# Eighteen more activation tiles of a two-block layer turned by the DMA crossbar

## The chip, the core and the metric

The kernel runs on one core of one Trainium2 chip. The metric is the device time of one execution in microseconds (us), the median of several. Each engine (PE = TensorE, ACT = ScalarE, DVE = VectorE, POOL = GpSimd, SP = SyncE, whose queue issues the DMAs) takes its instructions strictly in order and waits for the others by semaphores.

## The reference, cut to what matters

Two transformer-like blocks on 256 tokens of width 2048, all in float32.

```python
# first block: convolution + neighbourhood attention, then an MLP
proj = rms_norm(x, pre_mix_g) @ w_in                      # a, gate, q, k, v
mix  = concat([conv_group(a, gate), attention(q, k, v, rpb)]) @ w_out
x    = x + rms_norm(mix, post_mix_g)
f    = square(relu(rms_norm(x, pre_mlp_g) @ w_up)) @ w_down
x    = x + rms_norm(f, post_mlp_g)
# second block: mLSTM beside latent attention
proj = rms_norm_2(x, norm_g) @ w_in_2    # q_a,k_a,v_a,o_a,i_a,f_a,z_a,c_q,c_kv,k_r,z_b,g_a,g_b
qk_a = silu(causal_depthwise_conv(concat([q_a, k_a]), conv_w))      # 4 taps along tokens
h_a  = rms_norm_2(mlstm_chunkwise(q_a, k_a, v_a, i_a, f_a), mlstm_norm_g)
y_a  = (sigmoid(o_a) * h_a * silu(z_a)) @ w_a
q_b  = rope(rms_norm_2(rms_norm_2(c_q, q_lat_g) @ w_uq))
k_b, v_b = from(rms_norm_2(c_kv, kv_lat_g) @ w_ukv, k_r)
y_b  = (causal_attention(q_b, k_b, v_b) * silu(z_b)) @ w_b
y    = sigmoid(g_a) * y_a + sigmoid(g_b) * y_b
out  = x + y @ w_out_2
```

## The kernel before, in words

**Products.** Every large product has the activations (256 tokens, as two tiles of 128) stationary and streams weights. For float32 accuracy each operand is split in a high and a low part, and three products are added: `hi*whi`, `hi*wlo`, `lo*whi` (L594 to L596). The weights come in 732 units of 512 KB. A unit is loaded by SP into one of 4 buffers `raw` (L2215), ScalarE makes `whi` (L907), VectorE makes `wlo = raw - whi` (L1457), both in rings of 5, and TensorE multiplies the unit with 12 matmuls of 128x512 (two 128-row chunks, two token tiles, three products). A stripe is 512 output columns: 8 units where the sum runs over 2048 rows, 4 where over 1024.

**Order.** There is no scheduler at run time. Time is laid out in slots, two to a unit; `E("name")` is the slot in which stripe "name" has been summed. Each engine's program is made of generators ("sides"), one per kind of work; a side yields the slot at which its next piece stands, and the engine's program is the merge by slot. The splits of unit v stand at the slot in which unit v-5 has been multiplied (`slots_and_splits`, L507), since only then a place in the ring is free. So on VectorE and ScalarE an instruction that waits holds all splits behind it, and SP holds all loads behind a waiting transfer (a load of unit u+4 waits for the splits of unit u).

**Turning.** A stripe's result has tokens on the partitions, but the next product needs the features there. The tile is turned in 128x128 blocks. Most are turned on TensorE: `turn` (L569) makes four transposes (L573) into one PSUM bank, ScalarE reads the bank for the high part, VectorE for the low part. Only the 16 tiles of the MLP (`up`) are turned by the DMA crossbar, which takes 2-byte words: VectorE cuts the tile in its two 16-bit halves (L1720, two int16 copies), SP issues four DMA_TRANSPOSE (L2251), VectorE joins the halves (L1726, two int16 copies).

**The places concerned.** `qk2` are four stripes of 8 units, q_a and k_a of the mLSTM. Each is scaled by ScalarE (L883), turned, copied by ScalarE into `PRE` (L1160), convolved on VectorE (L1811 two and L1814 six instructions a pair of heads), passed through tanh (L1164) and combined (L1819). Beside it `row_side` works on the mLSTM's gates (VectorE L1840 to L1850, ScalarE L1183 to L1185). `ml` is the gated mLSTM result (4 tiles), `lat` the two latents, `ao` the attention's output (4 tiles), `yt` the sum of both branches (4 tiles, stripes `yb10` to `yb13` of 4 units each, the last product before `out0` to `out3`): VectorE adds the gated product (L2092, L2096), and makes the low part (L2102) from the turned tile.

Of the kernel before, what the change touches and what calls it, by code (L numbers as in the profile page):

```python
# [16 lines left out]
P = 128  # L17
# [170 lines left out]
def two_blocks(nc, d, out):  # L188
    with ExitStack() as ctx:
# [112 lines left out]
        PRE = [ar(12320 + 518 * i, 518).rearrange("p (k n) -> p k n", k=2) for i in range(2)]  # L302
        ROWS = [AR[0:8, 9260 + 256 * i:9516 + 256 * i] for i in range(9)]
# [12 lines left out]
        SG.append(ar(15360, 1024).rearrange("p (t n) -> p t n", t=2))  # L316
        at_p = [ar(16384 + 384 * i, 384) for i in range(3)]
# [39 lines left out]
        def sems(*names):  # L357
# [8 lines left out]
        ao_t, sm_t, row_t, row_n, ml_s, ml_o, ml_t = sems(  # L366
            "ao_t", "sm_t", "row_t", "row_n", "ml_s", "ml_o", "ml_t")
# [36 lines left out]
        yt_t = Later(x_t, 32)  # L404
# [120 lines left out]

        def na_parts():
# [13 lines left out]
        use += [(E(f"qk2{k // 2}") + 2 + 4 * (k % 2), "qk2", k) for k in range(8)]  # L540
        use += [(E(("cq", "ckv")[k // 2]) + 1 + k % 2, "lat", k) for k in range(4)]
        use += [(E(f"uqr{k // 2}") + 12 + 2 * (k % 2), "qr", k) for k in range(4)]
# [3 lines left out]
        use += [(AO0[k // 2] + 2 * (k % 2), "ao", k) for k in range(8)]  # L546
        TBK = {(name, k): 2 + i % 2 for i, (_, name, k) in enumerate(sorted(use))}
# [11 lines left out]
        def pe(e):  # L559
# [132 lines left out]
            def qk2_side():  # L692
                for n in range(4):
                    for pair in range(2):
                        yield E(f"qk2{n}") + 2 + 4 * pair
                        b = bank(TBK["qk2", 2 * n + pair], (qk2_p, 2 * n + pair + 1))
                        q.wait_ge(qk2_e, n + 1)
                        turn(b, SG[(0, 2, 3, 0)[n]], pair).then_inc(qk2_t.sem, 1)

# [24 lines left out]
            def ml_side():  # L724
                for n in range(4):
# [3 lines left out]
                    parts += [(ML0[2 * n + 1] + 8 + 2 * pair, "t", pair) for pair in range(2)]  # L729
                    for slot, part, h in sorted(parts):  # L730
# [8 lines left out]
                        elif part == "o":  # L739
# [8 lines left out]
                        else:  # L748
                            b = bank(h, (ml_h, 2 * n + h + 1), (ml_l, 2 * n + h + 1))
                            q.wait_ge(ml_x, 2 * n + 2)  # L750
                            turn(b, SG[n % 2], h).then_inc(ml_t, 1)

            def lat_side():
                for w, name in enumerate(("cq", "ckv")):
                    for pair in range(2):
                        yield E(name) + 1 + pair
                        b = bank(TBK["lat", 2 * w + pair], (lat_h, 2 * w + pair + 1), (lat_l, 2 * w + pair + 1))
                        q.wait_ge(lat_e, w + 1)
                        turn(b, SG[w], pair).then_inc(lat_t.sem, 1)
# [32 lines left out]
            def at_side():  # L792
                for slot, part, i in at_parts():
# [14 lines left out]
                    elif part == "t":  # L808
                        b = bank(1, (at_c, i + 1))
# [4 lines left out]
                    else:  # L814
                        b = bank(1, (at_x, i + 1))
# [7 lines left out]
            def ao_side():  # L823
                for n in range(4):
                    for pair in range(2):
                        yield AO0[n] + 2 * pair
                        b = bank(TBK["ao", 2 * n + pair], (ao_h, 2 * n + pair + 1), (ao_l, 2 * n + pair + 1))
                        q.wait_ge(at_x, 4 * n + 4)
                        turn(b, ZB[n % 2], pair).then_inc(ao_t, 1)

            def y_side():
                for n in range(4):
                    for pair in range(2):
                        yield E(f"yb1{n}") + 3 + pair
# [1630 lines left out]
```

## Time and profile before

| | us |
|---|---|
| median of 3 runs | 2162.8 (2161.03 to 2163.23) |
| the profiled execution's own time | 2163.23 |
| its span (first to last instruction) | 2161.4 |
| TensorE busy | 2148.8 (99%) |
| VectorE busy | 1382.7 (64%) |
| ScalarE busy | 1079.9 (50%) |
| splits on VectorE (L1457), 732 | 891.1 |
| splits on ScalarE (L907), 732 | 771.2 |
| transposes on TensorE (L573), 256 | 38.4 |

The busy time of an engine is what its instructions cover. Ends of matmuls are modelled and overlap, so the pace of TensorE is read from the starts of successive matmuls. The mean granted clock of TensorE is 0.998 of full speed. In the rows, an engine's name with q (SPq) is its queue of DMA issues; "[1.66 <-PE g L596]" behind a row is the idle time before it and what ended it. `arena` is one large tile of on-chip memory in which most buffers lie, `stage` are four staging tiles, `g` the PSUM sums, `s` the small PSUM banks.

### The profile page before, as it was taken

Reading aid. Unit: us, or ns where it says so; the run is one execution under the profiler, and the core shown is the slowest. Engines: PE = TensorE matmul, PEld = TensorE weight load, DVE = VectorE, ACT = ScalarE, POOL = GpSimd, SP = SyncE. Lnnn points to the kernel's source line nnn. Section 1 sums busy time; section 2 is a strip of 40 time slices with the busy share of each in tenths; the row PEclk is TensorE's granted clock in tenths of the full one; section 3 lists DMA queues with packets and bytes.
Section 4 is the critical chain, followed back from the end, with each engine's and each line's share of the span. In section 5 each row is a group of like instructions: output and inputs, shape, how many; then the busy total and the mean of one; then the engine's idle time right before and its main releaser. Section 6 shows DMA issues by size and latency. Waiting matters only on the chain.

```text
span 2161.4 us, 27345 instructions
## 1 busy us (share of the span) xinstructions
PE 2148.8 (99%) x9852; PEld 1777.6 (82%) x9852; DVE 1382.7 (64%) x1862; ACT 1079.9 (50%) x1503; POOL 60.2 (3%) x70
## 2 busy tenths in 40 slices
PE   9999999999999999999999999999999999999999
PEld 7888887888888888888788888888888888888887
DVE  6898857765665656656777445566445666666764
ACT  6544565654444444444575445554444655564442
POOL 1000100000000000000000000000000000000000
PEclk9999999999999999999999999999999999999999
DMA  9665446776766766767565765556666554555875
GB/s 328 183 189 165 145 144 213 211 214 199 234 199 209 214 202 202 212 189 218 165 207 186 222 193 176 176 162 201 201 202 202 177 184 146 175 176 181 323 238 165
DMA packets 152933, 428.29 MB, mean 198 GB/s; under 512 B 48216, under 2 KB 48736, under 8 KB 152544
## 3 DMA queue, kind: packets, MB, share of 16 engines
q1 hardware_dynamic: 150768, 420.64, 62.4%
q0 software_dynamic: 1744, 5.77, 0.8%
q8 instruction: 80, 1.31, 0.2%
q14 instruction: 53, 0.43, 0.1%
q10 hardware_dynamic: 288, 0.14, 0.0%
HBM read 407.60 MB, written 10.49 MB: 193 GB/s over the span
## 4 chain that ended last, share of the span: by engine, by line
PE 96%; DVE 2%; ACT 1%; issue 1%; DMA 0%; POOL 0%; ACTq 0%; DVEq 0%
PE g L594 30%; PE g L596 30%; PE g L595 30%; PE s L573 2%; PE s L651 1%; DVE wlo L1457 1%; PE s L805 0%; PE s L804 0%; DVE arena L1522 0%; DVE ta_lo L1634 0%; PE s L633 0%; PE s L643 0%; PE s L812 0%; PE s L689 0%; ACT whi L907 0%
## 5 line engine op out<-in xcount | busy, mean ns | idle before, releaser
L1457 DVE TENSOR_TENSOR wlo<-raw,whi 128x1024 fp32r<-128x1024 f32 x732 | 891.1, 1222 | 564.1 <-ACT whi L907 561.8
L907 ACT ACTIVATE whi<-raw 128x1024 fp32r<-128x1024 f32 x732 | 771.2, 1058 | 677.3 <-PE g L596 659.7
L594 PE MATMUL g<-whi,ta_hi 128*128 128x512 f32 x1920 | 762.9, 397 | 4.3 <-DVE wlo L1449 2.0
L596 PE MATMUL g<-whi,ta_lo 128*128 128x512 f32 x1920 | 749.3, 390 | 0.0
L595 PE MATMUL g<-wlo,ta_hi 128*128 128x512 f32 x1920 | 748.0, 390 | 0.0
L594 PEld LDWEIGHTS g<-whi,ta_hi 128*128 128x128 f32 x1920 | 360.9, 188 | 79.8 <-issue 6.0
L596 PEld LDWEIGHTS g<-whi,ta_lo 128*128 128x128 f32 x1920 | 360.8, 188 | 77.2
L595 PEld LDWEIGHTS g<-wlo,ta_hi 128*128 128x128 f32 x1920 | 361.4, 188 | 72.2
L594 PE MATMUL g<-whi,tb_hi 128*128 128x512 f32 x1008 | 397.8, 395 | 0.2 <-ACT arena L1096 0.2
L596 PE MATMUL g<-whi,tb_lo 128*128 128x512 f32 x1008 | 393.0, 390 | 0.0
L595 PE MATMUL g<-wlo,tb_hi 128*128 128x512 f32 x1008 | 392.6, 389 | 0.0
L596 PEld LDWEIGHTS g<-whi,tb_lo 128*128 128x128 f32 x1008 | 189.3, 188 | 40.1
L594 PEld LDWEIGHTS g<-whi,tb_hi 128*128 128x128 f32 x1008 | 189.6, 188 | 38.3 <-ACT arena L1096 0.5
L595 PEld LDWEIGHTS g<-wlo,tb_hi 128*128 128x128 f32 x1008 | 189.7, 188 | 38.1
L1522 DVE SCALAR_TENSOR_TENSOR arena<-arena,vc 128x256 f32<-128x256 f32 x240 | 101.6, 478 | 0.0
L2160 POOL TENSOR_TENSOR stat<-stat,ps 128x2 f32<-128x2 f32 (+3 forms) x24 | 34.2, 1426 | 1592.0 <-DVE stat L1472 712.6
L883 ACT ACTIVATE stage<-g,stat 128x512 f32<-128x512 f32 x60 | 38.0, 687 | 22.6 <-PE g L596 22.6
L1597 DVE TENSOR_TENSOR arena<-arena,g 128x512 f32<-128x512 f32 x64 | 41.3, 684 | 11.3 <-PE g L596 11.3
L888 ACT ACTIVATE stage<-g,stat 128x512 f32<-128x512 f32 x44 | 27.9, 685 | 26.8 <-PE g L596 24.3
L573 PEld LDWEIGHTS s<-cst,stage 128*128 128x128 f32 x256 | 31.4, 140 | 9.3 <-issue 0.9
L573 PE MATMUL s<-cst,stage 128*128 128x128 f32 x256 | 38.4, 272 | 0.3 <-issue 0.3
L1715 DVE TENSOR_TENSOR stage<-stage 128x1024 f32<-128x1024 f32 x16 | 19.6, 1225 | 26.3 <-ACT stage L1114 26.3
(226 smaller groups left out, 975.1 us busy)
## 6 DMA issues: line engine op xcount, KB each, us to landing
raw<-in_w_in SPq DMA_DIRECT2D x318, 512.0 KB, 4.1
raw<-in_w_up SPq DMA_DIRECT2D x128, 512.0 KB, 4.1
raw<-in_w_down SPq DMA_DIRECT2D x128, 512.0 KB, 4.1
raw<-in_w_out SPq DMA_DIRECT2D x64, 512.0 KB, 4.2
raw<-in_w_a SPq DMA_DIRECT2D x32, 512.0 KB, 4.2
raw<-in_w_b SPq DMA_DIRECT2D x32, 512.0 KB, 4.7
raw<-in_w_ukv SPq DMA_DIRECT2D x16, 512.0 KB, 4.3
raw<-in_w_uq SPq DMA_DIRECT2D x12, 512.0 KB, 3.6
```

The source lines that it names most:

```text
L573: ins = e.transpose(b[:, k * 256 + t * P:k * 256 + (t + 1) * P], src[:, t, c:c + P], ident)
L594: e.matmul(o, xh, wh, start=first, stop=False)
L595: e.matmul(o, xh, wl, start=False, stop=False)
L596: ins = e.matmul(o, xl, wh, start=False, stop=last)
L651: ins = e.matmul(b[:, h * 64:(h + 1) * 64], na_tb[i % 2][:, h * 256 + jt * P:h * 256 + (jt + 1) * P], V1[:, jt, pr * P + 64 * h:pr * P + 6 ...
L883: ins = e.activation(dst[:, t], gps[st.pair][t][:, 0:dst.shape[2]], ACT.Copy, scale=r[:, t:t + 1])
L888: ins = e.activation(dst[:, t], gps[st.pair][t][:, :], ACT.Tanh, scale=r[:, t:t + 1])
L907: e.activation(whi[u % RING][:, 0:n], raw[u % RAW][:, 0:n], ACT.Copy).then_inc(s_hi, 1)
L1457: e.tensor_tensor(l, r, h.bitcast(F32), ALU.subtract).then_inc(s_lo, 1)
L1522: e.scalar_tensor_tensor(CV[:, ct, :], UT[:, ct, j:j + 256], vec("w_dw", ct * 31 + j), CV[:, ct, :], ALU.mult, ALU.add).then_inc(cv, 1)
L1597: ins = e.tensor_tensor(f, f, gps[st.pair][t][:, :], ALU.add)
L2160: alone(e.tensor_tensor(r, v, half[:, 0:v.shape[1]], ALU.pow), rs_out, i + 1)
```

## The change

The tiles of qk2, ml, lat, ao and yt are turned by the crossbar too: 18 more jobs of four DMA_TRANSPOSE each. The tables `CBM` and `CBN` give each job its three buffers and its place in the order; `cut_words` and `join_words` are the two copies by VectorE. For qk2 the join is done by ScalarE, straight into `PRE`, in place of the copy from PSUM.

```diff
+        def cut_words(job, src):
+            for h in range(2):
+                e.tensor_copy(planes(CBM[job][0])[:, h], words(src)[:, h].rearrange("p (t n) -> p t n", t=2)).then_inc(
+                    w_cut.sem, 1)
+        def join_words(job):
+            q.wait_ge(d_turn, 64 * CBN[job] + 64)
+            for h in range(2):
+                e.tensor_copy(words(CBM[job][2])[:, h].rearrange("p (c n) -> p c n", c=4),
+                              turned(CBM[job][1])[:, h]).then_inc(w_join.sem, 1)
...
 # ScalarE, qk2
                     for pair in range(2):
-                        yield E(st.name) + 2 + 4 * pair
+                        yield E(st.name) + 8 + 4 * pair
-                        q.wait_ge(qk2_t, k + 1)
+                        q.wait_ge(d_turn, 64 * CBN["qk2", n] + 64)
...
-                        e.activation(pre[:, :, 3:259], two(bk), ACT.Copy).then_inc(qk2_p, 1)
-                        yield E(st.name) + 4 + 4 * pair
+                        for h in range(2):
+                            ins = e.activation(PRE_W[k % 2][:, h, :, 3:259], turned(CBM["qk2", n][1])[:, h, 2 * pair:2 * pair + 2],
+                                               ACT.Copy)
+                        ins.then_inc(qk2_p, 1)
+                        yield E(st.name) + 10 + 4 * pair
...
 # VectorE, qk2
+                    yield E(f"qk2{n}") + 1
+                    q.wait_ge(qk2_e, n + 1)
+                    q.wait_ge(d_turn, 64 * CBN["qk2", n])
+                    cut_words(("qk2", n), flat[(0, 2, 3, 0)[n]])
                     for pair in range(2):
-                        yield E(f"qk2{n}") + 2 + 4 * pair
+                        yield E(f"qk2{n}") + 8 + 4 * pair
...
 # VectorE, yt
                         if part == 1:
+                            yield E(st.name) + 1
+                            q.wait_ge(yb_s, k + 1)
+                            q.wait_ge(at_x, 16)
+                            q.wait_ge(d_turn, 64 * CBN["yt", n])
+                            cut_words(("yt", n), flat[2 + n % 2])
+                            yield E(st.name) + 7
+                            q.wait_ge(yt_h, 2 * n - 2)
+                            q.wait_ge(yt_l, 2 * n - 2)
+                            join_words(("yt", n))
+                            yield E(st.name) + 8
                             for pair in range(2):
-                                yield E(st.name) + 3 + pair
...
 # SP
-                for i in range(16):
-                    yield E(f"up{i // 2}{i % 2}") + 4
+                for job, j in CBN.items():
+                    name, n = job
+                    if name == "up":
+                        yield E(f"up{n // 2}{n % 2}") + 4
+                    elif name == "qk2":
+                        yield E(f"qk2{n}") + 4
+                    elif name == "ml":
+                        yield ML0[2 * n + 1] + ML_T[0]
+                    elif name == "lat":
+                        yield E(("cq", "ckv")[n]) + 4
+                        q.wait_ge(lat_q, 2 * n + 2)
+                    elif name == "ao":
+                        yield AO0[n] + AO_T[n][1]
+                    else:
+                        yield E(f"yb1{n}") + 3
+                    q.wait_ge(d_turn, 64 * j)
+                    q.wait_ge(w_cut, cut(job))
...
                     for h in range(2):
                         for t in range(2):
-                            e.dma_start_transpose(PT[:, h, :, t * P:(t + 1) * P], PL[:, h, t]).then_inc(d_turn.sem, 16)
+                            e.dma_start_transpose(to[:, h, :, t * P:(t + 1) * P], src[:, h, t]).then_inc(d_turn.sem, 16)
...
 # TensorE: qk2_side, lat_side, ao_side, y_side and the "t" parts of ml_side are gone (36 groups of four transposes)
-                        turn(b, SG[(0, 2, 3, 0)[n]], pair).then_inc(qk2_t.sem, 1)
-                            turn(b, SG[n % 2], h).then_inc(ml_t, 1)
-                        turn(b, SG[w], pair).then_inc(lat_t.sem, 1)
-                        turn(b, ZB[n % 2], pair).then_inc(ao_t, 1)
-                        turn(b, SG[2 + n % 2], pair).then_inc(yt_t.sem, 1)
```

The jobs of ml are cut 5 slots after the tile's last head has begun its scores, issued at +8, joined at +11 (`ML_T`); those of lat cut at E+1, issued at E+4, joined at E+8; those of ao by the table `AO_T`. Smaller edits go with it: the attention's second and third products alternate between two PSUM banks in place of one, the turns of the second `uqr` half stand four slots later, the load of the row sums stands at `E("qk23") + 16` in place of +10, and buffers that are now used by the crossbar bring waits on `ao_h`, `ao_l`, `w_cut` and `w_join`.

On VectorE at stripe `yb12` (stage0 and stage2 hold the gate and the sum, ta_lo the low part of the next product's activations), before:

```order
L2092 SCALAR_TENSOR_TENSOR stage0<-stage0,g10 128x512
L2092 SCALAR_TENSOR_TENSOR stage0<-stage0,g11 128x512
L2096 TENSOR_TENSOR stage2<-stage2,stage0 128x1024
L1457 TENSOR_TENSOR wlo4<-raw2,whi4 128x1024
L1457 TENSOR_TENSOR wlo0<-raw3,whi0 128x1024
L2102 SCALAR_TENSOR_TENSOR ta_lo<-s0,ta_hi 128x512
L2102 SCALAR_TENSOR_TENSOR ta_lo<-s1,ta_hi 128x512
L1457 TENSOR_TENSOR wlo1<-raw0,whi1 128x1024
L1457 TENSOR_TENSOR wlo2<-raw1,whi2 128x1024
L2092 SCALAR_TENSOR_TENSOR stage1<-stage1,g00 128x512
```

The same place on VectorE after (L1462 is the cut, L1469 the join, L1451 a split, L2154 the low part):

```order
L2134 SCALAR_TENSOR_TENSOR stage0<-stage0,g10 128x512
L2134 SCALAR_TENSOR_TENSOR stage0<-stage0,g11 128x512
L2138 TENSOR_TENSOR stage2<-stage2,stage0 128x1024
L1451 TENSOR_TENSOR wlo4<-raw2,whi4 128x1024
L1462 COPY arena<-stage2 128x1024 x2
L1451 TENSOR_TENSOR wlo0<-raw3,whi0 128x1024
L1451 TENSOR_TENSOR wlo1<-raw0,whi1 128x1024
L1451 TENSOR_TENSOR wlo2<-raw1,whi2 128x1024
L1469 COPY arena<-arena 128x1024 x2
L2154 SCALAR_TENSOR_TENSOR ta_lo<-arena,ta_hi 128x512 x2
L2134 SCALAR_TENSOR_TENSOR stage1<-stage1,g00 128x512
```

The cut stands one split later than the sum, the join behind the stripe's fourth split, and the low parts and the next stripe's sums stand behind the join. On SP at the same stripe after (raw are weight loads; before, the row of the transposes was not there and all else stood in this order):

```order
L2267 DMA raw2<-in_w_out_2 128x1024
L2267 DMA raw3<-in_w_out_2 128x1024
L2319 DMA_TRANSPOSE arena<-arena 128x4x128 x4
L2267 DMA raw0<-in_w_out_2 128x1024
L2267 DMA raw1<-in_w_out_2 128x1024
L2347 DMA stage1<-keep_gs 128x1024
```

The four transposes stand between the stripe's second and third load. On VectorE at the first qk2 stripe (arena 128x256 is the convolution, 8x256 the gates), before:

```order
L1457 TENSOR_TENSOR wlo0<-raw0,whi0 128x1024
L1811 TENSOR_SCALAR arena<-arena,vc 128x256 x2
L1814 SCALAR_TENSOR_TENSOR arena<-arena,vc 128x256 x6
L1457 TENSOR_TENSOR wlo1<-raw1,whi1 128x1024
L1819 SCALAR_TENSOR_TENSOR arena<-arena 128x512
L1457 TENSOR_TENSOR wlo2<-raw2,whi2 128x1024
L1811 TENSOR_SCALAR arena<-arena,vc 128x256 x2
L1814 SCALAR_TENSOR_TENSOR arena<-arena,vc 128x256 x6
L1457 TENSOR_TENSOR wlo3<-raw3,whi3 128x1024
L1819 SCALAR_TENSOR_TENSOR arena<-arena 128x512
```

and after (L1816, L1819 and L1824 are the same three lines, L1451 the split):

```order
L1451 TENSOR_TENSOR wlo0<-raw0,whi0 128x1024
L1462 COPY arena<-stage0 128x1024 x2
L1451 TENSOR_TENSOR wlo1<-raw1,whi1 128x1024
L1451 TENSOR_TENSOR wlo2<-raw2,whi2 128x1024
L1451 TENSOR_TENSOR wlo3<-raw3,whi3 128x1024
L1816 TENSOR_SCALAR arena<-arena,vc 128x256 x2
L1819 SCALAR_TENSOR_TENSOR arena<-arena,vc 128x256 x6
L1451 TENSOR_TENSOR wlo4<-raw0,whi4 128x1024
L1824 SCALAR_TENSOR_TENSOR arena<-arena 128x512
L1451 TENSOR_TENSOR wlo0<-raw1,whi0 128x1024
L1816 TENSOR_SCALAR arena<-arena,vc 128x256 x2
L1819 SCALAR_TENSOR_TENSOR arena<-arena,vc 128x256 x6
```

Both convolutions stand three splits later, the second one just ahead of the work on the gates.

## Rows read from the trace of the kernel before

**Rows 1.** The page: busy time, share of the span, instructions; then the chain's shares.

```profile
PE 2148.8 (99%) x9852; PEld 1777.6 (82%) x9852; DVE 1382.7 (64%) x1862; ACT 1079.9 (50%) x1503; POOL 60.2 (3%) x70
...
PE 96%; DVE 2%; ACT 1%; issue 1%; DMA 0%; POOL 0%; ACTq 0%; DVEq 0%
```

**Rows 2.** Timeline of TensorE, products alone: start, us, engine, line, operation, count.

```profile
1296.00 0.39 PE L594 MATMUL g<-whi,ta_hi 128*128 128x512 f32 x1
...
1307.56 0.39 PE L594 MATMUL g<-whi,ta_hi 128*128 128x512 f32 x1
```

**Rows 3.** Timeline of TensorE, a group of transposes and the products behind it.

```profile
2052.23 0.60 PE L573 MATMUL s<-cst,stage 128*128 128x128 f32 x4
...
2057.47 0.39 PE L594 MATMUL g<-whi,tb_hi 128*128 128x512 f32 x1
```

**Rows 4.** Groups of VectorE by shape: count, busy us, mean ns, idle before.

```profile
L1457 DVE TENSOR_TENSOR wlo<-raw,whi 128x1024 fp32r<-128x1024 f32 x730 | 889.4, 1223 | 563.9 <-ACT whi L907 561.8
L1726 DVE COPY arena<-arena 128x1024 int16<-128x1024 int16 x32 | 22.2, 751 | 1.1 <-DMA arena<-arena 1.1
L1720 DVE COPY arena<-stage 128x1024 int16<-128x1024 int16 x32 | 20.6, 688 | 0.0
...
L2102 DVE SCALAR_TENSOR_TENSOR ta_lo<-s,ta_hi 128x512 fp32r<-128x512 f32 x8 | 5.5, 693 | 4.7 <-ACT ta_hi L895 4.5
```

**Rows 5.** Timeline of ScalarE and VectorE, one unit's splits when nothing else is there.

```profile
2082.08 1.06 ACT L907 ACTIVATE whi<-raw 128x1024 fp32r<-128x1024 f32 x1 [1.66 <-PE g L596]
...
2083.17 1.23 DVE L1457 TENSOR_TENSOR wlo<-raw,whi 128x1024 fp32r<-128x1024 f32 x1 [1.50 <-ACT whi L907]
```

**Rows 6.** Three crossbar jobs: SP's queue, VectorE's join; then the page's landing time.

```profile
640.58 5.12 SPq L2251 DMA_TRANSPOSE arena<-arena  x4
...
879.94 6.29 SPq L2251 DMA_TRANSPOSE arena<-arena  x4
...
887.52 1.40 DVE L1726 COPY arena<-arena 128x1024 int16<-128x1024 int16 x2 [0.82 <-DMA arena<-arena]
...
966.56 0.33 SPq L2215 DMA_DIRECT2D raw<-in_w_down  x1
966.98 5.77 SPq L2251 DMA_TRANSPOSE arena<-arena  x4
...
974.02 1.40 DVE L1726 COPY arena<-arena 128x1024 int16<-128x1024 int16 x2 [0.28 <-DMA arena<-arena]
...
arena<-arena SPq DMA_TRANSPOSE x64, 3.3
```

**Rows 7.** Timeline of ScalarE, VectorE and TensorE in the first two qk2 stripes.

```profile
1097.85 1.27 ACT L883 ACTIVATE stage<-g,stat 128x512 f32<-128x512 f32 x2
...
1104.35 0.62 DVE L1811 TENSOR_SCALAR arena<-arena,vc 128x256 f32<-128x256 f32 x2 [3.03 <-DMA keep_x2s<-arena]
1104.88 2.46 DVE L1814 SCALAR_TENSOR_TENSOR arena<-arena,vc 128x256 f32<-128x256 f32 x6
...
1125.32 1.23 DVE L1457 TENSOR_TENSOR wlo<-raw,whi 128x1024 fp32r<-128x1024 f32 x1 [3.61 <-ACT whi L907]
...
1129.12 3.48 DVE L1457 TENSOR_TENSOR wlo<-raw,whi 128x1024 fp32r<-128x1024 f32 x3
...
1130.45 0.48 PE L594 MATMUL g<-whi,ta_hi 128*128 128x512 f32 x1
```

**Rows 8.** Timeline of VectorE at the second yb1 stripe, and that stretch by engine.

```profile
2034.67 1.28 DVE L2092 SCALAR_TENSOR_TENSOR stage<-stage,g 128x512 f32<-128x512 f32 x2 [0.34 <-PE g L596]
2035.99 1.23 DVE L2096 TENSOR_TENSOR stage<-stage 128x1024 f32<-128x1024 f32 x1
...
2034.60:2045.50 10.90, 10.90 (x54) 9.00 (x53) 8.03 (x9) 5.33 (x6) 0.00 (x0) 1.00 0.87 296
```

**Rows 9.** TensorE after a wait; the stretch by engine: PE, PEld, DVE, ACT, POOL, clock, DMA share.

```profile
260.07 1.97 PE L671 MATMUL s<-cst,arena 128*128 128x128 f32 x8 [1.98 <-DVE arena L1522]
...
260.10:263.50 3.40, 3.40 (x12) 3.06 (x13) 2.45 (x3) 2.02 (x3) 0.00 (x0) 0.50 0.28 80
```

More of the change, by code:

```diff
@@ L316, in two_blocks, with cut, join_of @@
         SG.append(ar(15360, 1024).rearrange("p (t n) -> p t n", t=2))
+        flat = [b[:, :] for b in STG] + [ar(15360, 1024)]
+        CBM = {}
+        for i in range(16):
+            CBM["up", i] = (ar(14576, 1024), ar(15600, 1024), ar(16624, 1024))
+        for n in range(4):
+            CBM["qk2", n] = (ar(15664, 1024), flat[(0, 2, 3, 0)[n]], None)
+        for n in range(4):
+            CBM["ml", n] = (ar(13360, 1024), flat[n % 2], ar(14384, 1024))
+        for w in range(2):
+            CBM["lat", w] = (ar(16384, 1024), ar(17408, 1024), ar(16384, 1024))
+        for n in range(4):
+            b = (flat[3], flat[4], flat[4], ar(10240, 1024))[n]
+            CBM["ao", n] = (b, ar(13312 + 1024 * (n % 2), 1024), b)
+        for n in range(4):
+            CBM["yt", n] = tuple(ar(4096 + 3072 * (n % 2) + 1024 * m, 1024) for m in range(3))
+        CBN = {job: i for i, job in enumerate(CBM)}
+        joined = [job for job in CBM if CBM[job][2] is not None]
+        def cut(job):
+            return 2 * CBN[job] + 2
+        def join_of(job):
+            return 2 * joined.index(job) + 2
         at_p = [ar(16384 + 384 * i, 384) for i in range(3)]
@@ L539, in two_blocks @@
         use += [(YA0[k // 2] + 2 * (k % 2), "ya", k) for k in range(4)]
-        use += [(E(f"qk2{k // 2}") + 2 + 4 * (k % 2), "qk2", k) for k in range(8)]
-        use += [(E(("cq", "ckv")[k // 2]) + 1 + k % 2, "lat", k) for k in range(4)]
-        use += [(E(f"uqr{k // 2}") + 12 + 2 * (k % 2), "qr", k) for k in range(4)]
+        use += [(E(f"uqr{k // 2}") + (12, 16)[k // 2] + 2 * (k % 2), "qr", k) for k in range(4)]
         use += [(E(f"uqn{k // 4}{k // 2 % 2}") + 2 + 2 * (k % 2), "uq", k) for k in range(8)]
@@ L545, in two_blocks @@
         use += [(E(f"ukn{k // 2}1") + 13 + k % 2, "kr", k) for k in range(4)]
-        use += [(AO0[k // 2] + 2 * (k % 2), "ao", k) for k in range(8)]
-        TBK = {(name, k): 2 + i % 2 for i, (_, name, k) in enumerate(sorted(use))}
+        TBK = {(name, k): 3 if slot >= AT0[0] else 2 + i % 2 for i, (slot, name, k) in enumerate(sorted(use))}
         UK, GB = (2, 3, 2, 3), (0, 1, 0, 1)
@@ L814, in at_side @@
                     else:
[L815 removed]
+                        b = bank(1 + i % 2, (at_x, i + 1))
                         q.wait_ge(at_c, i + 1)
@@ L1227, in ml_side @@
                         parts += [(ML0[h], "e", h), (ML0[h] + 4, "q", h)]
-                    parts += [(ML0[2 * n + 1] + 8 + 2 * pair, "t", pair) for pair in range(2)]
+                    parts += [(ML0[2 * n + 1] + ML_T[2], "t", pair) for pair in range(2)]
                     for slot, part, h in sorted(parts):
@@ L1281, in zb_side @@
                     if n == 0:
-                        q.wait_ge(lat_t, 4)
+                        q.wait_ge(w_cut, cut(("lat", 1)))
                         q.wait_ge(lat_q, 4)
@@ L1870, in ml_side @@
                         parts += [(ML0[h], "a", h), (ML0[h], "s", h), (ML0[h] + 4, "x", h), (ML0[h] + 4, "y", h)]
-                    parts += [(ML0[2 * n + 1] + 8 + 2 * pair, "t", pair) for pair in range(2)]
+                    parts += [(ML0[2 * n + 1] + 5, "u", n), (ML0[2 * n + 1] + ML_T[1], "v", n)]
+                    parts += [(ML0[2 * n + 1] + ML_T[2] + 1, "w", pair) for pair in range(2)]
                     for slot, part, h in sorted(parts):
@@ L2293, in out_side @@
             def out_side():
-                after = ((kr_t, 4), (yb_s, 7), (yb_s, 8), (yt_t, 6))
+                after = ((ao_l, 8), (yb_s, 7), (yb_s, 8), (w_cut, cut(("yt", 2))))
                 for n in range(4):
```

221 lines of the change are left out of this document (113 added, 108 removed).

## The prediction, made before the changed kernel was run

> **What bounds the kernel now.** The page first: TensorE is busy for 2148.8 of 2161.4 us and the chain of waits is 96% TensorE [rows 1]. So what TensorE is spared comes off the time one for one, unless something else becomes late; the question is what the other engines have in hand. For that I read three more things. The timeline of TensorE gives its pace: from 1296.00 to 1307.56 lie 51 matmuls, 0.2267 us each, a unit of 12 is 2.72 us and a stripe of four units 10.9 [rows 2]. The timeline of the splits gives the lead of the weights: ScalarE's split of a unit starts when a ring place comes free (released by TensorE), takes 1.06, VectorE's takes 1.23 and ends 2.3 us after [rows 5]; four units stand ahead, so a unit is ready 10.9 - 2.3 - 0.1 = 8.5 us before it is used. That is all the delay VectorE may have without TensorE noticing. The groups by shape show VectorE idle before splits only for ScalarE's half [rows 4]: it has room on average (1382.7 us of work), but it is in order, so a wait there holds every split behind it.
>
> **What goes.** 36 groups of four transposes. From 2052.23 (a group) to 2057.47 lie 21 matmuls: 5.24 us where 21 x 0.2267 = 4.76 would do, so a group costs 0.48 us [rows 2, 3]. 36 x 0.48 = 17.3 us off TensorE. The two reads of a bank go too, but reads of the joined tile replace them at the same size (on ScalarE 0.64, as two of 128x512 took 1.27 [rows 7]; on VectorE 0.69 [rows 4]).
>
> **What comes, per job.** VectorE: two cuts of 0.69 and two joins of 0.75 [rows 4], 2.8 us (1.3 in pairs for qk2, whose join is ScalarE's). SP: four transposes whose issue takes 5.12 us when nothing hinders, 5.77 and 6.29 seen [rows 6]. After the last issue the data took 887.52 - 886.23 = 1.29 and 974.02 - 972.75 = 1.27 us to reach the waiting join [rows 6]. I take 5.12 + 1.28 = 6.4 us from the first issue to the join ("the turn"). Bounds: 5.1, if the landing were hidden in the issue; 7.6, the longer whole job seen (887.52 - 879.94); between them 7.1 (3 issues of 1.28, then the median landing of 3.3). The other 14 jobs say only that they landed before VectorE asked (1.1 us of idle in 32 joins [rows 4]). A group of transposes gave its bank in 0.60 us [rows 3], so each of these tiles is some 8 to 10 us later than before, with cut and join.
>
> **yt, the four stripes of yb1.** Before, VectorE has 8.0 us of work in each 10.9 us [rows 8]. Now its order from one join to the next is: join 1.40, ScalarE's first high part 0.64, two low parts 1.4, the gated products 1.28 and the sum 1.23 of the next stripe, a split 1.2, cut 1.3, a second split 1.2 (it frees the load that stands ahead of the transposes on SP), then the turn 6.4: 1.4 + 0.7 + 1.4 + 1.3 + 1.2 + 1.2 + 1.3 + 1.2 + 6.4 = 16.1, with 0.4 for that load's issue and less some overlap 16.3 us [rows 4, 6, 8]. The two remaining splits lie under the turn. TensorE wants a stripe every 10.9, so each falls back by 5.4 us. Count from the end of TensorE's work on yb10: the first join ends at 14.4 (2.5 for product and sum, 3.6 for split, cut, split, 0.4 load issue, 6.4 turn, 1.5 join), the others at 30.8, 47.2 and 63.5. The split after the next stripe's sums, needed by TensorE at 21.8, is ready at 20.2: lead 1.6, nothing lost. One period on it is ready at 36.5, wanted at 32.6: 3.9 us lost. The third at 52.8, wanted at 47.4 (shifted by the first loss): 5.5. Then `out0` needs the last tile's high and low parts, ready at 63.5 + 0.7 + 0.7 and a hand-over = 65.0, for its seventh unit, wanted at 58.3: 6.7. Together 16.1 us. At a turn of 5.1 it is 10.9, at 7.6 20.9: 4 us per us of turn, since three waits in a row carry it.
>
> **qk2.** Each of four stripes has 8 units = 21.8 us for: copies 1.3, cut 1.3, two splits, turn 6.4, ScalarE's join, convolution, tanh, combine, and again. No row shows ScalarE on int16; by its 1.27 for two of 128x512 from PSUM [rows 7], less a little from on-chip memory, two make 1.15; half of that (0.6) or 1.4, as VectorE's, would shift each stripe by under 0.6. A convolution is 3.0 us (1104.35 to 1107.34 [rows 7]). In the first stripe the copies end at 1099.1 [rows 7], the cut behind two splits at 1102.5; SP issues at 1104.1, behind the load that waits for the next split; landed 1110.5, joined 1111.7. So the convolution starts at 1111.7 instead of 1104.35, the second one, behind a combine, two splits and ScalarE's next join (ordered behind its own work on the gates), at 1119.0. Behind it stand the gates' rows: two (0.8), a split, the combine 0.7, two more 0.8, then the wait of 3.61 for ScalarE seen at 1125.32 (the gates' activations and a split), then 2.6 of rows up to 1129.12 [rows 7]. Before, the split of that unit (the 387th) ended at 1126.55 and was used at 1130.45: lead 3.9 [rows 7]. Now 1122.0 + 0.8 + 0.4 + 1.15 + 0.65 + 0.8 = 1125.8, + 3.6 + 1.2 = 1130.7, while TensorE, spared its transposes, asks at 1129.2: 1.5 lost. The next split has the 2.6 of rows ahead: 1.0 more. The second stripe catches up (no gates), lead down to 0.2. In the third and fourth, from the low split before the cut to the one after the first convolution: cut 1.2 + split 1.1 + turn 6.4 + join 1.15 + convolution 3.0 + split 1.2, 14.1 us for four units (10.9); with the second convolution 24.2 for the stripe's 21.8, so 2.4 and some tenths each, 2.5 and 2.6. Together 7.6 us; 2.5 at a turn of 5.1, 12.4 at 7.6.
>
> **ml, lat, ao.** Same three costs, but the tiles are wanted many units later and other splits lie between cut and join. By the same count the smallest lead left is about 1 us, at lat's second tile, 5 us at ml: no loss; up to 3 us if that turn is 1.5 us longer and the attention's rows pile up. Their VectorE work (10 x 2.8 us) lies in idle time. `up` is unchanged. The second bank for attention takes away waits of TensorE, but all its idle is 2161.4 - 2148.8 = 12.6 us [rows 1], mostly at both ends: 0, at most 1 gained.
>
> **Clock.** After an idle of 1.98 us TensorE ran at a granted 0.50 for 3.4 us (1.2 instead of 2.4 GHz) [rows 9]: 1.7 us lost if nobody waits. Here waits of 2.5 to 6.7 us come seven times, but after most of them the splits, not TensorE, set the pace, and a slow TensorE uses up time that it would wait anyway. Only after the last yt wait is it lost in full: +2, bounds 0 and 4.
>
> **Sum.** 2163.2 (the profiled execution's own time, 0.4 above the median; the sum starts from it and is compared with runs like the median's) - 17.3 + 7.6 + 16.1 + 2 = 2171.6; less the 0.4: 2171.
>
> **Rivals.** One: nothing waits, because the leads of 8.5 us cover the joins everywhere and only the transposes count: 2162.8 - 17.3 = 2146. For it: DVE is busy 64% only and the same scheme costs `up` 1.1 us of waiting. Against: `up` has 8 units between tiles, yb1 has 4, and 16.4 does not go into 10.9. Two: the turn is short (5.1): stalls of 2.5 + 10.9, no clock loss, 2159. Against: both jobs in which VectorE waited show the 1.28. Three: the turn grows by queueing. The yb1 stripes had the DMA engines busy 0.87 [rows 8]; jobs of 7.6 were seen. Then 12.4 + 20.9 + 2 - 17.3 on 2163: 2181, and every further 0.5 us adds 4. Against: in the stalled stage the loads come every 16.4 us, not 10.9, which thins the load.
> Four: issues are cheap. If a transpose were issued like a load, 0.33 as at 966.56 [rows 6], the turn would be 3 issues of 0.4 and the 2.56 from the last issue to its landing (1.28 + 1.28), 3.8, and only yt's period (13.7) too long: 5.8 lost, 2163.2 - 17.3 + 5.8 = 2152. The Trainium skill says "TRN2 transpose DMAs are as fast as regular DMAs" (Advanced Engine Details and Errata, X-Bar Transpose (TRN2)). The trace doesn't agree as to the issue: 1.28 us against 0.33.
>
> **Chances.** The forecast 0.56, its own range 2166 to 2178; no waits 0.12; the short turn 0.10; the long turn 0.15; cheap issues 0.07. The difference this kernel's measurement can tell is about 0.2%, 4.3 us: faster is under 2158.5, slower over 2167.1. Faster: 0.12 + 0.07 + half of the short turn = 0.24. Same: the other half and the low edge of the forecast, 0.10. Slower: 0.66. The range leaves out the case without waits and the far end of the long turn: 2152 to 2183.
>
> **What would show it.** L573 has 112 transposes in place of 256. In the last 140 us VectorE idles before its joins, 3 to 5 us each, put down to the DMA, and TensorE waits three times for a split or a low part, 4 to 7 us each; the joins lie about 16 us apart. Around 1130, 1175 and 1200 of the before's time TensorE waits for `wlo`, 1 to 2.5 us. Wrong would be: joins 11 us apart (then the turn is short or the lead enough, and the time is near 2150), a wait of TensorE in ml, lat or ao, or a turn over 7.6.

## The result and the profile after

The changed kernel took 2184.97 us (median of 4 runs, 2184.26 to 2188.34), the kernel before 2162.0; the ratio is 1.0109 with a 95% interval of 1.0092 to 1.0127. So it is slower by 1.1%, 23 us where 9 were forecast, and lies just outside the range (2183). The profiled execution is the longest of the four, 2188.34 with a span of 2186.5; it is compared below with the profile of before (2163.23), a difference of 25.1. What is read from this one trace can therefore be some us more than the medians show.

The page's first rows answer to [rows 1]: busy time per engine, then the granted clock in 40 slices.

```profile
span 2186.5 us, 27242 instructions
...
PE 2143.9 (98%) x9708; PEld 1769.7 (81%) x9708; DVE 1416.9 (65%) x1926; ACT 1081.9 (49%) x1511; POOL 61.1 (3%) x70
...
PEclk9999999999999999999999999999999999999989
```

TensorE has 144 matmuls fewer. It is busy 42.6 us short of the span, where before it was 12.6. The table of waits says what it waited for: consumer, releaser, us in total, times, longest.

```profile
PE g L626 <- DVE wlo L1451: 8.5, 4, 2.7
PE g L626 <- ACT whi L898: 7.4, 2, 3.9
PE g L626 <- DVE ta_lo L2154: 6.5, 1, 6.5
PE s L605 <- ACT stage L877: 3.6, 1, 3.6
...
PE g L626 <- DVE tb_lo L1455: 2.0, 1, 2.0
...
PE s L736 <- ACT ps L1168: 1.4, 1, 1.4
```

The first three rows are qk2 and yt, as forecast. The other three were not in the prediction: the scaled copies of `uqn10`, the low part of ml's last tile, and the gates' transposed values, each held up behind a join in ScalarE's or VectorE's order.

**yt.** Timeline of VectorE behind the first and second join (L1469 join, L2154 low part, L2134 and L2138 the next stripe's sums, L1462 cut), and the last join; then SP's four issues. They answer to [rows 6] and [rows 8].

```profile
2057.13 1.38 DVE L1469 COPY arena<-arena 128x1024 int16<-128x1024 int16 x2 [2.49 <-DMA arena<-arena]
2059.20 1.29 DVE L2154 SCALAR_TENSOR_TENSOR ta_lo<-arena,ta_hi 128x512 fp32r<-128x512 f32 x2 [0.70 <-ACT ta_hi L1409]
2060.41 1.28 DVE L2134 SCALAR_TENSOR_TENSOR stage<-stage,g 128x512 f32<-128x512 f32 x2
2061.73 1.23 DVE L2138 TENSOR_TENSOR stage<-stage 128x1024 f32<-128x1024 f32 x1
2062.87 1.22 DVE L1451 TENSOR_TENSOR wlo<-raw,whi 128x1024 fp32r<-128x1024 f32 x1
2064.00 1.29 DVE L1462 COPY arena<-stage 128x1024 int16<-128x1024 int16 x2
2065.21 3.49 DVE L1451 TENSOR_TENSOR wlo<-raw,whi 128x1024 fp32r<-128x1024 f32 x3
2073.38 1.38 DVE L1469 COPY arena<-arena 128x1024 int16<-128x1024 int16 x2 [4.69 <-DMA arena<-arena]
...
2107.64 1.36 DVE L1469 COPY arena<-arena 128x1024 int16<-128x1024 int16 x2 [6.45 <-DMA arena<-arena]
```

```profile
2066.95 5.13 SPq L2319 DMA_TRANSPOSE arena<-arena  x4
...
2083.19 5.12 SPq L2319 DMA_TRANSPOSE arena<-arena  x4
...
2099.43 6.91 SPq L2319 DMA_TRANSPOSE arena<-arena  x4
```

The joins stand 16.25 us apart (2057.13, 2073.38, 2089.62), 16.3 by the sum, and 6.43 behind the first issue. The last one came after 8.21. TensorE's three waits, first matmul behind each:

```profile
2080.55 0.77 PE L626 MATMUL g<-whi,ta_hi 128*128 128x512 f32 x1 [3.85 <-ACT whi L898]
...
2096.68 0.47 PE L626 MATMUL g<-whi,ta_hi 128*128 128x512 f32 x1 [3.58 <-ACT whi L898]
...
2110.54 0.77 PE L626 MATMUL g<-whi,ta_hi 128*128 128x512 f32 x1 [6.52 <-DVE ta_lo L2154]
```

**The clock.** Stretches of 3.4 us behind the last yt wait and behind the first wait of qk2 (answer to [rows 9]): us, busy of PE, PEld, DVE, ACT, POOL, clock, DMA share, GB/s.

```profile
2110.50:2113.90 3.40, 3.36 (x8) 2.72 (x9) 3.23 (x4) 2.53 (x3) 0.00 (x0) 0.50 0.27 54
1133.00:1136.40 3.40, 2.98 (x12) 2.18 (x12) 3.26 (x6) 2.63 (x4) 0.00 (x0) 1.00 0.49 154
```

Behind 6.52 us of waiting the clock was 0.50 (1.2 GHz), behind 2.72 it stayed 1.00 (2.4 GHz), yet behind ml's wait of 1.97 it fell to 0.50.

**ml and ao**, the places where no loss was forecast. VectorE at ml's last tile, then ScalarE at ao's second tile (L1400 is its high part, L877 the copies of uqn10) and TensorE's transposes that wait for them:

```profile
1496.68 1.39 DVE L1469 COPY arena<-stage 128x1024 int16<-128x1024 int16 x2 [4.15 <-DMA stage<-arena]
1500.80 1.23 DVE L1451 TENSOR_TENSOR wlo<-raw,whi 128x1024 fp32r<-128x1024 f32 x1 [2.73 <-ACT whi L898]
1501.94 1.67 DVE L1455 SCALAR_TENSOR_TENSOR tb_lo<-arena,vc,tb_hi 128x256 fp32r<-128x256 f32 x4
```

```profile
1869.36 1.15 ACT L1400 ACTIVATE tb_hi<-arena 128x512 fp32r<-128x512 f32 x2 [4.93 <-DVE arena L1469]
...
1872.79 1.25 ACT L877 ACTIVATE stage<-g,stat 128x512 f32<-128x512 f32 x2
```

```profile
1874.18 0.63 PE L605 MATMUL s<-cst,stage 128*128 128x128 f32 x4 [3.58 <-ACT stage L877]
```

**qk2.** ScalarE's joins (L1151), the first and the last, with the wait before them:

```profile
1112.57 1.41 ACT L1151 ACTIVATE arena<-stage 128x512 int16<-128x512 int16 x2 [5.44 <-DMA stage<-arena]
...
1199.27 1.42 ACT L1151 ACTIVATE arena<-stage 128x512 int16<-128x512 int16 x2 [7.34 <-DMA stage<-arena]
```

The first transposes were issued at 1104.30 (1104.1 by the sum), but landed 8.27 later; those of the fourth stripe after 7.94, the middle ones after 6.39 and 6.79.

### The profile page after: what moved, and what is told of

Same layout as the page of the kernel before. It is cut to its first block and busy times, and to the rows that moved or that the text cites. A ratio compares the mean times of both kernels' runs of the same rounds, so it can differ in the third digit from the quotient of the medians.

```text
span 2186.5 us, 27242 instructions
## 1 busy us (share of the span) xinstructions
PE 2143.9 (98%) x9708; PEld 1769.7 (81%) x9708; DVE 1416.9 (65%) x1926; ACT 1081.9 (49%) x1511; POOL 61.1 (3%) x70
## 5 line engine op out<-in xcount | busy, mean ns | idle before, releaser
L1451 DVE TENSOR_TENSOR wlo<-raw,whi 128x1024 fp32r<-128x1024 f32 x732 | 888.2, 1221 | 512.0 <-ACT whi L898 510.0
L1469 DVE COPY arena<-arena 128x1024 int16<-128x1024 int16 x50 | 34.7, 750 | 30.8 <-DMA arena<-arena 30.8
L877 ACT ACTIVATE stage<-g,stat 128x512 f32<-128x512 f32 x60 | 37.8, 685 | 17.4 <-PE g L628 17.4
L1462 DVE COPY arena<-stage 128x1024 int16<-128x1024 int16 x60 | 38.6, 685 | 0.0
```

The source lines that it names most:

```text
L877: ins = e.activation(dst[:, t], gps[st.pair][t][:, 0:dst.shape[2]], ACT.Copy, scale=r[:, t:t + 1])
L1451: e.tensor_tensor(l, r, h.bitcast(F32), ALU.subtract).then_inc(s_lo, 1)
L1462: e.tensor_copy(planes(CBM[job][0])[:, h], words(src)[:, h].rearrange("p (t n) -> p t n", t=2)).then_inc(w_cut.sem, 1)
L1469: e.tensor_copy(words(CBM[job][2])[:, h].rearrange("p (c n) -> p c n", c=4), turned(CBM[job][1])[:, h]).then_inc(w_join.sem, 1)
```

## The experiments

Theory 1: the crossbar is cheap for TensorE and the loss is in-order waiting; joins stand at places in the orders of VectorE and ScalarE where their data cannot be there, and hold the splits behind them. Theory 2: the crossbar, the DMA queues or VectorE's added work are the limit wherever the joins stand. Each kernel is the changed one with the edit shown, unless it says otherwise.

**yt_later**

```diff
 # ScalarE            -  yield E(f"yb1{n}") + 8     +  yield E(f"yb1{n}") + 11
 # VectorE, a side of its own for join and low part
-                            yield E(st.name) + 7
+                    yield E(f"yb1{n}") + 10
-                            yield E(st.name) + 8
+                    yield E(f"yb1{n}") + (12, 12, 12, 11)[n]
```

SP's transposes stay at E+3; since a tile is now joined after the next one is issued, SP waits for the join of two tiles before, not of the last one (the buffers alternate).

> Only the places of the four yt jobs are moved: VectorE's join from E+7 to E+10, ScalarE's high part from E+8 to E+11, the low part from E+8 to E+12 (E+11 for the last). The transposes stay at E+3. Theory 1 (the loss is in-order waiting: a join placed before its data hold the splits behind it): joins start without a wait, 10.9 us apart; of the 19.5 us that the trace shows around units 702, 706 and 708, 1 to 3 are left, all at the last tile, which out0 needs at once. Time 2185 - 17.5 = 2167 (2165 to 2170). Theory 2 (the crossbar or the DMA queues are the limit at this load, so that stripes 10.9 us apart only make the turns longer): turns over 8 us, joins still wait, time above 2175.

Measured: 2172.98 (2169.01 to 2173.91), 12.0 less. The joins no longer wait, except the last: VectorE in the third stripe,

```profile
2061.11 1.38 DVE L1469 COPY arena<-arena 128x1024 int16<-128x1024 int16 x2
2062.37 1.21 DVE L1451 TENSOR_TENSOR wlo<-raw,whi 128x1024 fp32r<-128x1024 f32 x1
2063.50 1.29 DVE L2157 SCALAR_TENSOR_TENSOR ta_lo<-arena,ta_hi 128x512 fp32r<-128x512 f32 x2
```

and of three waits of TensorE one is left, 3.1 us. Theory 1 holds for the first two; the last tile costs more than I said, 5.0 us around it (3.1 of waiting, 1.7 at half clock behind it), and so the time is 3 us over the range expected. Its turn was a usual one here, 6.46 us: the place alone is too late for `out0`.

**qk2_later**

```diff
-                        yield E(st.name) + 8 + 4 * pair        # ScalarE's join; VectorE's convolution likewise
+                        yield E(st.name) + ((11, 17), (11, 15), (11, 15), (11, 15))[n][pair]
-                yield E("qk23") + 16
+                yield E("qk23") + 19
```

> Only qk2 is moved: ScalarE's joins and the convolutions from E+8 and E+12 to E+11 and E+15 (E+11 and E+17 in the first stripe, behind the gates' work), tanh and combine two slots behind, the load of the row sums from E(qk23)+16 to +19. Theory 1: of the 13.9 us that units 380 to 410 lose against the kernel before (1.4 at the gates' transpose, 2.7 + 0.8, 2.5 and 2.5 waiting for splits, 1.7 + 1.5 at half clock, and the rest), 1 to 3 are left: 2185 - 12 = 2173 (2171 to 2175). Theory 2 (VectorE's work in the stripe, 18 of 21.8 us, bunches wherever it is put): half of it stays, 2178.

Measured: 2172.02 (2170.91 to 2173.27), 13.0 less. Of TensorE's waits in qk2 0.3 us is left, and none at the gates. Theory 1 holds, with 1 us more than expected.

**ml_ao_later**

```diff
-        ML_T = (8, 11, 12)
+        ML_T = ((8, 13, 14), (8, 13, 14), (8, 13, 14), (7, 12, 13))
-        AO_T = ((-1, 1, 6), (-1, 1, 6), (1, 3, 17), (-1, 2, 7))
+        AO_T = ((-1, 1, 6), (-1, 1, 9), (1, 3, 17), (-1, 2, 8))
```

> Only ml and ao are moved: ml's joins from +11 to +13, high and low parts two later, and for the last tile the transposes one slot earlier (+7), join +12; ao's second join from +5 to +8, its last from +6 to +7. Theory 1: the two waits of TensorE that the prediction did not have (1.97 us for ml's last low part at 1503 and 3.6 us for the scaled copies of uqn10 at 1874, each with 1.7 to 2.0 us at half clock behind it) go: 2185 - 8 = 2177 (2175 to 2179). Theory 2: they are only moved on to the next consumer: within 2 us of 2185.

Measured: 2177.97 (2177.94 to 2179.87), 7.0 less; of the 3.6 us wait 1.2 is left, of ml's nothing. The two places that the prediction priced at nothing cost 7.

**all_later**: the three edits together, and lat's:

```diff
-                    yield E(name) + 8       # join, high part, low part: + 8, + 9, + 10
+                    yield E(name) + 11      # + 11, + 12, + 13
```

> All of the moves together, and those of lat (join E+11, high +12, low +13). Theory 1: the losses are separate waits and add: 2185 - 17.5 - 12 - 8 = 2147.5 (2145 to 2151), 36 x 0.48 = 17.3 us under the kernel before less 1 to 4 us of waits that are left. Theory 2 (crossbar turns cost something wherever they stand, by DMA load or VectorE's extra 2.8 us a job): above 2155.

Measured: 2151.1 (2148.76 to 2152.63); against the kernel before the ratio is 0.9952 (0.9935 to 0.9968), faster. That is at the upper end of what was expected (2151). The three gains sum to 32.0, together (with lat's move, never run alone) they are 33.9: separate waits that add, within the 1 to 2 us by which each median is uncertain. What is left at TensorE:

```profile
PE g L626 <- DVE ta_lo L2157: 2.3, 1, 2.3
...
PE s L605 <- ACT stage L877: 1.2, 1, 1.2
```

Theory 2 falls: the same crossbar work, the same copies, and 34 us less.

**yt_by_tensor**: the four yt jobs taken out of the crossbar's table, TensorE, ScalarE and VectorE as in the kernel before.

```diff
-        for n in range(4):
-            CBM["yt", n] = tuple(ar(4096 + 3072 * (n % 2) + 1024 * m, 1024) for m in range(3))
```

> The changed kernel with the four yt tiles turned by TensorE as before; all else stays. Theory 1 (the stages are independent): the difference to the kernel before is 9.5 us when yb1 begins and stays so, no wait at units 702 to 708: 2162.6 + 9.5 = 2172. Theory 2 (the stages earlier only used up a lead that a later one would have lost too): over 2176 or under 2168.

Measured: 2169.24 (2166.46 to 2172.36, 5 runs). 15.7 less, and eight groups of transposes came back (3.8): yt's waits and half clock cost 19.5 us. The distance to the kernel before is the same from yb1's start to the end, so the lead that earlier stages use up is not missed later; it was 6.0 us in this trace, not the 9.5 expected, because qk2 and ml lost less in it, and so the time is 3 us under theory 1's 2172.

**yt_twice**

```diff
+                    if name == "yt":
+                        other = turned(ar(11264, 1024))
+                        for h in range(2):
+                            for t in range(2):
+                                e.dma_start_transpose(other[:, h, :, t * P:(t + 1) * P], src[:, h, t]).then_inc(d_turn.sem, 16)
```

The counts in the waits for `d_turn` grow with it.

> The changed kernel with each yt job's four transposes preceded by four more of the same source into a buffer that nobody reads. Theory 1 (each of four turns in a row stands in VectorE's order, 4 us of time for each us of turn): turns of 6.4 + 5.1 = 11.5 us, joins 21.4 us apart, 2185 + 4 x 5.1 = 2205 (2203 to 2208). Theory 2 (part of a turn is covered): the extra transposes cost less, 2185 + 10 to 15.

Measured: 2207.61 (2204.83 to 2210.78), 22.6 more, and the joins stand 21.44 apart:

```profile
2084.11 1.36 DVE L1472 COPY arena<-arena 128x1024 int16<-128x1024 int16 x2 [9.92 <-DMA arena<-arena]
...
2105.55 1.36 DVE L1472 COPY arena<-arena 128x1024 int16<-128x1024 int16 x2 [9.90 <-DMA arena<-arena]
```

From the first issue to the join the four turns took 5.65, 5.24, 5.23 and 5.45 us more than in the changed kernel, 21.6 together, for 22.6 us of time. So yt's price is 4 us for each us by which every turn grows; at a last turn of 8.2 instead of 6.4 the sum's 16.1 becomes 17.9, and with 1.8 at half clock behind it 19.7: the 19.5 measured.

**filler and filler_2** (the clock). Useless matmuls ahead of seven waits:

```diff
+            def fill(b, T, n):
+                for _ in range(n):
+                    e.matmul(b[:, 0:512], T[:, 0, 0:P], T[:, 0:2, :].rearrange("p a n -> p (a n)"), start=True, stop=True)
+                if j == 0 and u in FILL:
+                    fill(bank(3), tb_hi if u > 600 else ta_hi, FILL[u])
```

> The changed kernel with matmuls of no use put ahead of seven of TensorE's waits, each some 1 us shorter than the wait: 8 before units 402 and 410, 6 before 512, 12 before the first transposes of uqn10, 13, 17 and 24 before units 702, 706 and 708 (128x512, into a free bank, read by nobody). Theory 1 (behind a wait TensorE runs at half clock for a time): the granted clock stays 1.00 behind them; saved are 1.7 and 1.5 in qk2 (they delay the stripe's end, and so the next turn), 1.7 at 512, 2.0 at uqn10 and 1.8 at 708, while at 702 and 706 the splits set the pace and nothing is won: 2185 - 8.7 = 2176. Theory 2 (the 1.7 us behind each wait come from late splits, not from the clock): no change or slower, 2185 or more.

Measured: 2185.39 (2182.51 to 2187.19), no gain. In the profile the clock is full behind five of the seven. The third qk2 stripe of filler, by engine:

```profile
1179.00:1182.40 3.40, 3.40 (x15) 2.84 (x16) 3.31 (x8) 2.51 (x4) 0.00 (x0) 1.00 0.54 171
```

Behind the other two, where 2.5 and 2.9 us of waiting were left, it fell as before. So the clock is nearly as theory 1 said and the time is not; hence the second kernel. Two things cover the effect: ml's last turn took 8.37 us (6.46 in the changed kernel), and the useless matmuls outlasted two of the waits, by 1.7 us at unit 708 and 0.7 at uqn10.

> As filler, with more of the useless matmuls (10, 10, 12, 14, 15, 24, 25), since in filler two of the seven places still waited 2.5 and 2.9 us behind them and ran at half clock. Theory 1a (the half clock costs where nothing later waits on VectorE's chain of its own): full clock behind all seven, and against 2185 a gain of 3 to 5 us (qk2 about 2, ml or ao about 1, the last yt wait 1.8), the rest being given back in the next wait, whose end VectorE sets. Theory 1b (it costs everywhere): 8 us gained. Theory 2 (the turns' own scatter, 6.4 to 8.4 us, hides all of it): within 2.5 us of 2185, with waits that are longer by what the clock gave.

Measured: 2185.19 (2184.75 to 2189.19). Again no gain, with waits of 1.6 us or less behind the useless matmuls. But at uqn10 the standstill of the useful work grew by 4.5 us: ao's second turn took 8.13 us (6.37 in the changed kernel), and the useless matmuls, which had to wait for their bank first, began at half clock and ran 2.7 us past the moment at which the scaled copies were there.

```profile
1869.46 5.06 PE L612 MATMUL s<-ta_hi 128*128 128x512 f32 x14 [3.17 <-ACT arena L1321]
1874.36 0.60 PE L605 MATMUL s<-cst,stage 128*128 128x128 f32 x4
```

So this place does not test the clock. In yt the trace does: with the clock kept full, the useful work stood still for 5.4 us ahead of unit 706 (0.2 of it behind useless matmuls that ran on), 3.7 in the changed kernel, at the same turn (6.45 and 6.43). What the clock gave, the next wait took, as theory 1a says of these waits; 1b falls there. For the whole time, between 1a (3 to 5 us) and 2 (the scatter of the turns hides it) the two runs do not decide: the scatter, 6.4 to 8.4 us a turn, is as large as the effect.

**gap**, made from the kernel before: the clock's price with nothing else late.

```diff
+                    q.wait_ge(gapk, 8 * GAPU.index(u) + 8)      # TensorE, ahead of 8 units
+                    for m in range(8):                          # GpSimd, once the unit before is multiplied
+                        e.memset(gap_t[:, :], 0.0).then_inc(gapk.sem, 1)
```

> The kernel before with eight waits put into TensorE (ahead of units 410, 418, 426, 434, 708, 712, 716, 720): each waits for GpSimd to have done eight small memsets of its own, begun when the unit before was multiplied, some 3 us. Theory 1 (the clock): behind each wait TensorE runs at 0.50 for about 3.4 us and loses 1.7, so the time grows by the eight waits and 13.6 us more. Theory 2 (the loss in the changed kernel came from splits that were late too): it grows by the eight waits alone.

Measured: 2191.28 (2190.83 to 2192.41), 30.3 more than before. Two of the eight waits and the stretches behind them:

```profile
1197.50 0.75 PE L603 MATMUL g<-whi,ta_hi 128*128 128x512 f32 x1 [2.59 <-POOL gapt L2166]
...
2119.86 0.50 PE L603 MATMUL g<-whi,ta_hi 128*128 128x512 f32 x1 [2.59 <-POOL gapt L2166]
```

```profile
1197.50:1200.90 3.40, 3.40 (x8) 2.72 (x9) 0.91 (x1) 0.00 (x0) 0.00 (x0) 0.51 0.74 263
...
2119.90:2123.30 3.40, 3.40 (x15) 2.82 (x16) 0.00 (x0) 0.33 (x1) 0.00 (x0) 1.00 0.66 225
```

The same wait of 2.6 us was followed by a clock of 0.51 in one place and 1.00 in the other. The wait is the same each time (2.6 us between modelled ends, 2.8 by the starts of the matmuls). Against the same matmuls of the kernel before, the two units behind the wait took 1.7 us more in four of the eight places and 0.13 in the other four; all eight waits together are 22.1 us, the rest of the 30.3 is 8.2, 1.0 us a wait, and four times 1.7 with four times 0.13 are 7.3 of it. Theory 1 in part: a wait can cost half clock, with nothing else late, but not each wait does.

**all_later_2 and last_by_tensor** (for a faster version). First, three more places moved:

```diff
-                        yield E(f"yb1{n}") + 3                    # SP
+                        yield E(f"yb1{n}") + (3, 3, 3, 2)[n]
-                            q.wait_ge(d_turn, 64 * CBN["yt", n])
+                            q.wait_ge(d_turn, 64 * CBN["yt", n] - 64 * (n > 0))
-        AO_T = (..., (-1, 1, 9), ...)
+        AO_T = (..., (-1, 0, 11), ...)
```

> all_later with three further places: the last yt tile's transposes at E+2 instead of E+3 and its cut no longer waiting for the transposes of the tile before (other buffer), ao's second tile issued one slot earlier, its join and parts behind uqn10's scaled copies (+10, +11). Theory 1: the waits of 2.3 us (last low part at 2072) and 1.2 us (copies of uqn10 at 1853) go: 2151 - 3.5 = 2147.5, 0.7% under the kernel before. Theory 2: the last one is only moved, as the low part comes 10 us after the sum whatever is done: 2149 to 2151.

Measured: 2151.57 (2148.38 to 2152.65), no change against all_later. ao's second tile gained 0.4 (a wait of 0.8 for 1.2). The last yt tile was issued 2.9 us earlier, counted from its stripe's sum, and took 9.5 us instead of 7.0, so its join came only 0.4 earlier; and TensorE's wait was 3.0, no longer for the low part but for a split:

```profile
2061.09 5.99 SPq L2324 DMA_TRANSPOSE arena<-arena  x4
...
2071.87 1.06 ACT L898 ACTIVATE whi<-raw 128x1024 fp32r<-128x1024 f32 x1 [3.68 <-DMA raw<-in_w_out]
...
2074.94 0.47 PE L626 MATMUL g<-whi,ta_hi 128*128 128x512 f32 x1 [2.99 <-ACT whi L898]
```

With the transposes one load further ahead on SP, the next weights were issued at 2067.18 only, and ScalarE's split waited for them, with the tile's high part and another split behind it. So theory 2's number came, by another way than it says: the move put the loads late. That tile goes back to TensorE:

```diff
-        for n in range(4):
+        for n in range(3):
             CBM["yt", n] = tuple(ar(4096 + 3072 * (n % 2) + 1024 * m, 1024) for m in range(3))
+                    turn(b, SG[3], pair).then_inc(yt_t.sem, 1)    # TensorE, E("yb13") + 3 + pair
```

> all_later_2 with the last yt tile alone turned by TensorE. Theory 1 (that tile cannot be hidden: out0 wants it 16.3 us after its sum begins, and it needs 14.4 to 19 us by the crossbar): two groups cost 0.95, the wait of 2.3 to 3.0 us and 1.2 to 1.9 lost around it go, 2151.6 - 3 = 2148.5. Theory 2: the earlier three tiles' turns (8.0 to 9.0 us from the first issue there) reach the wait instead: 2151.

Measured: 2147.29 (2146.01 to 2148.58, 5 runs), ratio 0.9934 (0.9922 to 0.9947): theory 1 holds, and the kernel is faster than both, 0.7% under the one before. Its page:

```profile
span 2145.4 us, 27250 instructions
...
PE 2132.1 (99%) x9716; PEld 1763.3 (82%) x9716; DVE 1415.2 (66%) x1922; ACT 1084.9 (51%) x1511; POOL 61.2 (3%) x70
```

The span is again TensorE's busy time and 13.3 us. 34 groups fewer than before at 0.48 are 16.3 us; by the ratio 14.3 were had.

## Why the direction was right and the size wrong

The forecast was 2171, the measured time 2185. Of the 14 us between, 7.0 lie in ml and ao, which were priced at nothing, 5.4 in qk2 (13.0 for 7.6) and 1.4 in yt with the clock behind it (19.5 for 18.1).

**The transposes removed (17.3): right.** Where nothing else changed, each tile takes 0.95 us off the distance between the two traces, two groups of 0.48, in ml's first tiles and yt's first as in all_later. In the best version 14.3 of 16.3 us arrive.

**The turn (6.4): right as the usual value, wrong as the only one.** Of the 16 turns in the changed kernel's second block whose join waited, nine took 6.35 to 6.52 us, the others 6.8 to 8.3. The prediction took the scatter as a rival ("the turn grows by queueing") with one price for all; it is each turn by itself. It bears on the sum at qk2's first and last tile (8.27, 7.94) and yt's last (8.21).

**yt (16.1): mechanism right.** Period 16.25 by the trace for 16.3; waits at units 702, 706 and 708 as named. yt_by_tensor gives 19.5 for the stage: 16.1, 1.8 for the last turn, 1.8 for the clock behind it. That the total came so close has some luck in it: the waits were 3.9, 3.6 and 6.5 for 3.9, 5.5 and 6.7, with a long last turn in the third.

**qk2 (7.6): mechanism right, too small.** The forecast waits were there (2.7, 0.8, 2.5, 2.5 us for 1.5, 1.0, 2.5, 2.6), and two things beside them: TensorE waited 1.4 us for the gates' values, which ScalarE makes behind the join, and the clock took 1.7 each behind the third and fourth stripe's waits. qk2_later gives 13.0. ScalarE's joins took 1.41 a pair, not 1.15.

**ml, lat, ao (0): the step that failed.** The prediction counted the lead of the weights there, and that was enough: no wait for `wlo` at all, and none of TensorE in lat. It did not count the other things that stand behind a waiting join: ml's last low part behind join, high part and a split, wanted by `ya0` at once; and the scaled copies of `uqn10`, behind ao's high part on ScalarE, wanted by TensorE's own transposes. ml_ao_later puts both at 7.0 us, clock included, with 1.2 us of waiting still there.

**The clock (2): too small.** The sum charged it behind the last yt wait alone, arguing that elsewhere the splits set the pace. That is right in yt (the second wait was 3.6 instead of 5.5, the half clock of the first used up in it; in filler_2, with the clock kept, the standstill was 5.4), and wrong in qk2, ml and ao. Behind the fourth stripe's wait of qk2 and behind ml's the next two units took 1.7 us more than in the kernel before, behind uqn10's 1.6, and the distance between the two traces stayed within 0.1 us of its new value for the 20 units that follow. In the profile the clock fell behind seven waits; so many the prediction named too ("waits of 2.5 to 6.7 us come seven times"), but its own list has five of that size (2.5, 2.6, 3.9, 5.5 and 6.7); the other two were ml's and uqn10's.

Summed anew from the runs: 2162 - 17.3 + 19.5 (yt) + 13.0 (qk2) + 7.0 (ml, ao) = 2184.2, for 2185.0 measured. The three terms are differences of measured medians, each uncertain by 1 to 2 us, and qk2_later and ml_ao_later leave small waits in; that the sum closes to 1 us is partly luck.

**The rivals.** No waits is out by the joins' waits. Cheap issues is out: four transposes held SP for 5.12 us as before. The short turn is out: no join that waited came under 6.35 us behind its first issue. The long turn was right for some jobs.

## What to carry to other kernels

A transfer that takes the place of a matmul moves the work off the bound engine, but its latency goes to whoever joins its result, and on an in-order engine to everything behind that instruction. Lay the join where its data surely are, issue early but not ahead of a load that is wanted soon (all_later_2), and ask of every wait not only whether the main stream has lead, but what else is queued behind it on that engine and who wants that next. Where the consumer comes at once (the last tile before the next product), keep the fast path, even on the bound engine.

## What the runs showed that was not expected

A wait of TensorE of 2.6 us was followed by half clock in four of eight like places, at 1.7 us each, and by full clock in the other four (gap). In the changed kernel it stayed full behind 2.7 us and fell behind 2.45 and 1.97; in all_later it was full throughout, behind 2.31 too. What decides is left open.

A crossbar job of the same size took 6.35 us from first issue to join in the best case, and up to 8.4 where the join waited for it (once 9.5, in all_later_2); part of it is issue (5.12 to 6.9 us for four), part landing: of the two longest in qk2 one had an issue of 5.17 us. The cause of the scatter was not found.
